# First layer's last attention pair: memory rows rounded at steps 13 to 18, one weight piece's rest on GpSimd in quarters, the out-projection begun at steps 28 and 30

## What is computed

```
mkv  = rms_norm(mem) @ w_mem_kv[0]                 # 256 memory tokens, 4 heads of 64
proj = rms_norm(h) @ w_in_a[0]                     # c_q, c_kv, k_r, q_m, gate
main = mla_mixer(c_q, c_kv, k_r, positions, ...)   # 12 heads, causal, in 128-query blocks
mem_out = memory_attention(q_m, k_m, v_m)          # 4 heads, every token sees all 256
y = concatenate([main, mem_out]) * silu(gate)      # 512 x 1024
h = h + rms_norm(y @ w_out[0], norm_post[0])       # the out-projection
```

## Time and profile before

| | us |
|---|---|
| median of the runs | 1177.34 (1177.16 to 1177.47) |
| the profiled execution | 1177.3 |
| its span | 1175.5 |
| first layer's sweep, last pair and tail | 218 to 242 |

### The profile page before, as it was taken

The page is one execution under the profiler, slowest core; times in us unless marked ns, Lnnn a source line. Parts: engine busy times, 40 slices in busy tenths (PEclk is TensorE's granted clock), DMA queues, the critical chain, the costliest instruction groups (busy, mean ns, idle before and its releaser), DMA issues.

```text
span 1175.5 us, 16031 instructions
## 1 busy us (share of the span) xinstructions
PE 1159.8 (99%) x5967; PEld 913.6 (78%) x5967; DVE 546.6 (47%) x997; ACT 596.8 (51%) x1256; POOL 459.4 (39%) x331
## 2 busy tenths in 40 slices
PE   8999999999999999999999999999999999999998
PEld 7988866678987666668888886887666677888886
DVE  4311487826011655545567556502787750033333
ACT  7444677755344655555545653634556552343242
POOL 6534732143344222233344332445444443444461
PEclk9999999999999999999999999999999999999999
DMA  8533311223335322113232322333222113322321
GB/s 300 149 106 69 69 23 48 73 77 84 93 90 138 93 62 86 55 61 81 77 99 79 93 67 60 90 89 104 59 54 54 55 55 90 100 98 90 108 90 72
DMA packets 111573, 100.99 MB, mean 86 GB/s; under 512 B 21168, under 2 KB 98300, under 8 KB 111496
## 3 DMA queue, kind: packets, MB, share of 16 engines
q1 hardware_dynamic: 108952, 95.38, 28.0%
q0 software_dynamic: 864, 3.15, 0.7%
q10 hardware_dynamic: 1680, 1.44, 0.4%
HBM read 97.83 MB, written 2.12 MB: 85 GB/s over the span
## 4 chain that ended last, share of the span: by engine, by line
PE 94%; ACT 2%; DVE 1%; DMA 1%; issue 1%; POOL 1%; SPq 0%; DVEq 0%; ACTq 0%
PE bank L607 50%; PE bank L2074 8%; PE bank L1732 7%; PE bank L1524 6%; PE bank L878 4%; PE bank L896 3%; PE bank L912 3%; PE bank L2090 2%; PE bank L2102 2%; PE bank L1301 2%; PE bank L2114 2%; PE bank L1821 1%; DMA w_raw<-in_w_mem_kv 1%; PE bank L717 1%; PE bank L1316 1%
## 5 line engine op out<-in xcount | busy, mean ns | idle before, releaser
L526 POOL TENSOR_TENSOR w_lo<-w_raw,w_hi 128x1024 fp32r<-128x1024 f32 (+4 forms) x157 | 353.0, 2249 | 623.4 <-ACT w_hi L511 623.4
L511 ACT ACTIVATE w_hi<-w_raw 128x1024 fp32r<-128x1024 f32 (+6 forms) x161 | 159.3, 990 | 228.1 <-PE bank L607 202.8
L607 PE MATMUL bank<-acts_hi,w_hi 128*128 128x512 f32 (+1 forms) x576 | 224.0, 389 | 1.0 <-POOL w_lo L526 1.0
L607 PE MATMUL bank<-acts_lo,w_hi 128*128 128x512 f32 (+1 forms) x576 | 222.5, 386 | 0.0
L607 PE MATMUL bank<-acts_hi,w_lo 128*128 128x512 f32 (+1 forms) x576 | 222.5, 386 | 0.0
L607 PEld LDWEIGHTS bank<-acts_hi,w_hi 128*128 128x128 f32 x576 | 108.2, 188 | 24.5 <-POOL w_lo L526 1.5
L607 PEld LDWEIGHTS bank<-acts_lo,w_hi 128*128 128x128 f32 x576 | 108.2, 188 | 22.0
L607 PEld LDWEIGHTS bank<-acts_hi,w_lo 128*128 128x128 f32 x576 | 108.2, 188 | 21.3
L2209 DVE TENSOR_TENSOR_SCAN arena_end<-arena,junk 128x512 f32<-128x512 f32 (+3 forms) x64 | 72.5, 1133 | 58.6 <-ACT arena L2159 58.6
L607 PE MATMUL bank<-w_hi,acts_hi 128*128 128x512 f32 (+4 forms) x240 | 87.0, 362 | 0.3 <-POOL w_lo L526 0.3
L607 PE MATMUL bank<-w_hi,acts_lo 128*128 128x512 f32 (+4 forms) x240 | 86.2, 359 | 0.0
(11 more groups left out here) (308 smaller groups left out, 2147.1 us busy)
## 6 DMA issues: line engine op xcount, KB each, us to landing
w_raw<-in_w_in SPq DMA_DIRECT2D x64, 512.0 KB, 3.7
w_raw<-in_w_out SPq DMA_DIRECT2D x24, 512.0 KB, 3.6
w_raw<-in_w_in_b SPq DMA_DIRECT2D x22, 512.0 KB, 3.9
w_raw<-in_w_in_a SPq DMA_DIRECT2D x10, 512.0 KB, 4.0
w_raw<-in_w_mem_kv SPq DMA_DIRECT2D x8, 512.0 KB, 8.4
w_raw<-in_w_sb_proj SPq DMA_DIRECT2D x8, 512.0 KB, 3.4
w_raw<-in_w_ssd_proj SPq DMA_DIRECT2D x8, 512.0 KB, 3.5
arena_shared<-f_kept_rows SPq DMA_DIRECT2D x11, 256.0 KB, 4.5
```

The source lines that it names most:

```text
L511: nc.scalar.activation(w_at(p)[0][:, 0:size], w_raw[p % RAW][:, 0:size], ACT.Copy).then_inc(w_high.sem, 1)
L526: nc.gpsimd.tensor_tensor(lo[:, 0:size], w_raw[p % RAW][:, 0:size], hi[:, 0:size].bitcast(F32), ALU.subtract).then_inc(w_rest.sem, 1)
L607: mm = nc.tensor.matmul(bank_of(S, s, g)[0:lhs.shape[1], 0:rhs.shape[1]], lhs, rhs, start=j + kk + t == 0, stop=j == len(S.pieces) - 1 and ...
```

## The change

- `gated_high` and `gated_low` of the memory pairs move: ScalarE makes them at the end of steps 13 and 17, VectorE at the end of steps 14 and 18.
- Piece 1 of `pA_out` leaves `rest_on_dve`: its rest is on GpSimd again. The rests of the pieces from the third of `pA_qk` to piece 1 of `pA_out` are each made by four instructions of a quarter of the columns; the last one counts.
- `begin_out` takes a list of (piece, row), and stands at step 28 (piece 0, first row), 30 (piece 0, second row), 32 (piece 1, first row) and 33 (piece 1, second row), behind the step's other work. The second layer calls it as before.

```diff
+        in_quarters = set()
...
-            nc.gpsimd.tensor_tensor(lo[:, 0:size], w_raw[p % RAW][:, 0:size], hi[:, 0:size].bitcast(F32),
-                                    ALU.subtract).then_inc(w_rest.sem, 1)
+            parts = 4 if p in in_quarters else 1
+            for n in range(parts):
+                to = slice(n * size // parts, (n + 1) * size // parts)
+                ins = nc.gpsimd.tensor_tensor(lo[:, to], w_raw[p % RAW][:, to], hi[:, to].bitcast(F32), ALU.subtract)
+            ins.then_inc(w_rest.sem, 1)
...
                 if s < steps:
                     turn_in(counts(s))
-                elif s < steps + 2:
-                    begin_next(s - steps)
+                begin_next(s)
...
-        def begin_out(pe, S, A, j):
-
-            pe.wait_ge(w_rest.sem, S.piece0 + j + 1)
-            wh, wl = (w[:, 0:2 * S.width].rearrange("p (k n) -> p k n", k=2) for w in w_at(S.piece0 + j))
-            for kk in range(2):
+        def begin_out(pe, S, A, parts):
+
+            for j, kk in parts:
+                pe.wait_ge(w_rest.sem, S.piece0 + j + 1)
+                wh, wl = (w[:, 0:2 * S.width].rearrange("p (k n) -> p k n", k=2) for w in w_at(S.piece0 + j))
                 pe.wait_ge(*A.low(2 * j + kk + 1))
...
+        EARLY_ROWS = (13, 17)
+        OUT_STEPS = {28: ((0, 0),), 30: ((0, 1),), 32: ((1, 0),), 33: ((1, 1),)}
...
-                for c in {1: (0, 1), 2: (2,), 3: (3,)}.get(s - last, ()):
+                for c in {EARLY_ROWS[0]: (0,), EARLY_ROWS[1]: (1,), last + 2: (2,), last + 3: (3,)}.get(s, ()):
                     gated_high(act, attA, c)
...
-                if s == last:
-                    dve.wait_ge(C["product"].sem, pA_qk.done_after(0, pA_qk.n - 1, 0))
-                if s == last:
-                    rest_dve(dve, pA_out.piece0 + 1)
-                if s == last + 1:
-                    gated_low(dve, attA, 0)
-                    gated_low(dve, attA, 1)
+                if s - 1 in EARLY_ROWS:
+                    gated_low(dve, attA, EARLY_ROWS.index(s - 1))
...
-        rest_on_dve.update(S.piece0 + 1 for S in (pA_out, pB_out))
+        rest_on_dve.add(pB_out.piece0 + 1)
...
+        for S, next_S in ((pA_qk, pA_out),):
+            in_quarters.update(range(S.piece0 + 2, next_S.piece0 + 2))
```

More of the change, by code:

```diff
@@ L1348, in mla_pe @@
             pe.wait_ge(*pA_qr.evac(MB))
-            sweep_pe(pe, attA, turn_in, counts, beside, lag=2, bank_free=pA_v.evac(2 * MB), begin_next=lambda j: begin_out(pe, pA_out, attA, j))
+            sweep_pe(pe, attA, turn_in, counts, beside, lag=2, bank_free=pA_v.evac(2 * MB), begin_next=lambda s: begin_out(pe, pA_out, attA, OUT_STEPS.get(s, ())))
         def head_of_step(s):
@@ L1535, in counts @@
                 return 0
-            sweep_pe(pe, attB, turn_in, counts, lag=2, second=(pB_gate.evac(2 * MB), (sem["gates_in"], 1)), begin_next=lambda j: begin_out(pe, pB_out, attB, j))
+            sweep_pe(pe, attB, turn_in, counts, lag=2, second=(pB_gate.evac(2 * MB), (sem["gates_in"], 1)), begin_next=lambda s: begin_out(pe, pB_out, attB, {32: ((0, 0), (0, 1)), 33: ((1, 0), (1, 1))}.get(s, ())))
         def fox_act(act):
```

## The result

The changed kernel takes **1180.55 us** (median of 8 runs, 1179.68 to 1181.44) against 1177.46 us (1177.16 to 1178.42) for the kernel before, measured alongside: a ratio of 1.0025, 95% interval 1.0016 to 1.0034. It is slower by 3.1 us. I had predicted 1179.1 us and a range from 1177.2 to 1180.3.

The account below looks back on a forecast made before the run. TensorE, busy for 1159.8 of 1175.5 us, was taken as the bound, any new wait a full loss. 0.75 + 0.47 + 0.6 = 1.8 us on 1177.34 gave 1179.1 us, range 1177.2 to 1180.3.

Parts of the forecast that it names:

- Step A: Memory rows' low parts moved on VectorE to steps 14 and 18: 0.38 us stall each, +0.75 us for two.
- The first rival: The rows cost nothing at steps 14 and 18, as TensorE waits for another copy: 1178.4 us, chance 0.20.
- Step B: Rest of weight piece 1 moved from VectorE to GpSimd: two scalings wait for quarters, step 30 starts 0.47 us later.
- The fourth rival: Quarters don't let VectorE in: first scaling waits for the fourth quarter, 1.5 us for 0.47; 1180.1 us, chance 0.06.
- The second rival: GpSimd's next quarter always goes first: scalings wait 0.71 us each, steps 14 and 18 stall 0.60; 1180.5 us, chance 0.15.
- Step C: Out-projection begun at steps 28, 30, 32, 33: filler and pair 2's low part delay the tail, +0.6 us.
- The trap: At step 32 TensorE needs pair 2's low part ahead of step 33's transposes: gap of 1.5 to 2 us.
- The third rival: VectorE alone held the tail, so relieving it closes both TensorE gaps: a gain, 1175.7 us, chance 0.09.

Follow-up runs that it names:

- A alone: Kernel before with only the memory rows' parts moved to steps 13, 14, 17 and 18: 1178.62 us, +1.36.
- C alone: Kernel before with the out-projection's new order and low parts at the end of steps 13 and 17, rests whole: 1177.93 us.
- the attempt at a faster order: Kernel before with low parts at the end of steps 13 and 17 and one out-projection group drawn forward to step 28: 1177.05 us against 1177.17.

## Why the prediction was wrong

The mechanisms of all three steps were the right ones, and the prices of B and C were right within 0.2 us. Two steps failed. Step A was mis-sized, so that every execution pays 2.3 us where the sum said 1.8; that alone ends at 1179.8 us, the median of the lower four executions, inside the range. And the wait at step 32 (step C) was priced without the clock that falls behind it: 1.57 us in half of the executions, a term that the prediction didn't have, and the one that brought the median out of the range.

**Step A, mis-sized: 0.75 predicted, 1.22 measured.** The step that failed is the slack. I took the first copy to end at 189.26, gave the transposes 0.29 us of slack, and put 0.04 us on the signal between the two, for which no row shown there speaks. In the changed kernel the copy ends near 189.90 (189.41 + 0.49) and the transposes start at 190.03, so the way from one to the other takes 0.13 us. The experiments show that transposes which wait for the copy start 0.62 to 0.63 us behind its start; in the earlier trace rows they start 0.78 us behind it. So the slack was 0.15 to 0.16, not 0.29: the copy's 0.64 less 0.16 is the 0.48 us by which the transposes moved. The missing 0.13 us is the other half: the four transposes take 0.79 for 0.64 us. The weight load of the second two comes at 190.38, 0.60 us behind the second copy's start near 189.78, as that of the first two (190.00) comes 0.59 behind the first copy's; the profile names no releaser here, so that they wait for the second copy is read from these two distances. I had named that ("no slack, as the second transposes may see it") and made it only the bound. The row of the copies in the earlier trace rows is two merged into one, and I reckoned with the first of them alone. The 0.61 a place is my upper bound of 0.60 for no slack. The first rival (A is free) falls; it would be right one step earlier, where the same subtraction costs nothing.

**Step B: 0.47 predicted, 0.34 in the changed kernel, 0.25 alone.** The scalings' delays are 0.03 and 0.28 us for 0.11 and 0.36. The fourth rival (quarters don't let VectorE in) falls; it is what happens with the whole piece, 1.32 us. The second rival had the end of 1180.5 us, which is nearly the time measured, but not by its mechanism: it wanted both scalings to wait 0.71 us. Only its size at steps 14 and 18 (0.60 each) came true.

**The rule that I weighed there.** VectorE's subtraction beside the 64-column quarters took 0.69 us, and 0.68 at the end of step 13 with no GpSimd beside it: it didn't wait. GpSimd did, 1.61 us for four quarters that take 1.16 where VectorE's subtraction isn't beside them. Beside the 256 columns in one piece VectorE took 0.81. The rule of the Trainium skill (SBUF — State Buffer, Who interferes with whom), by which one of the two waits for the other's whole instruction, fits the direction of all three. The size fits less well: in A alone VectorE's subtraction started 0.26 us before GpSimd's ended (186.58 for 186.84) and took 0.12 longer. My conclusion from it, that VectorE would be the one to wait at step 14, was wrong for the changed kernel: A rose above 0.9, but through the copies.

**Step C: 0.6 predicted, 0.77 measured** (0.73 alone). The trap was where the prediction put it: the scores of step 31 at 235.24, the low part 3.37 us later (predicted 3.34), the last value matmuls 2.83 us behind its start (predicted 2.74), and a wait of 1.63 us (1.5 to 2 predicted). The prediction's 1.09 less B's 0.47 is 0.62; those 0.03 and 0.09 make 0.74 of the 0.77. The third rival, the gain, falls twice: C alone costs 0.73, and the attempt at a faster order gains nothing that can be told from no change.

**What had no step: the clock.** The prediction foresaw the wait and priced it only as time in which TensorE does nothing. 9 of the change's 17 executions took some 1.5 us longer, and the one of them that was profiled shows the clock at 1.2 GHz behind the wait. That moved the median of the eight runs from 1179.8 to 1180.55 us, over the upper edge of the range. Moving one entry from step 32 to step 33 takes the upper group away (none in 11 executions), and the others gain 0.3 us.

## What to carry to other kernels

A merged row of two copies has two ends, and a consumer that needs both has the slack of the later one; price a step that is inserted into a full chain at its whole slot unless each of those ends has room. Look for the engine's idle time one step up or down before inserting it: the same subtraction cost 0.61 us at one step and nothing at the one before. When a new order makes TensorE wait long in one piece, price the clock behind it too, and run such a kernel often enough to see both groups.

## What the runs showed of the hardware

- TensorE's clock fell from 2.4 to 1.2 GHz for 3.4 us behind a single wait of 1.63 us, in a kernel in which TensorE is busy for 99% of the time. Two profiles show it (the second at 1.64 us); by time and mean clock it happened in 15 of 39 executions, and in none of 77 without a wait over 1.2 us behind the kernel's start. The price is 1.54 and 1.57 us, about as much as the wait. The Trainium skill (TensorE: Matmul & The Clock Gate, Part 1) says that the gate's rhythm runs free of the kernel, which would explain why executions of one kernel differ; no run here can show it.
- A scaling of 0.35 us alone on VectorE took 1.32 us beside one GpSimd subtraction of 1024 columns, and two of them took 0.38 and 0.62 beside the same work in quarters. The quarters cost GpSimd 2.89 us for 2.37, 0.17 us for each further instruction.
